# Triangular 16x16 blocks turned onto partitions and solved by VectorE, behind the attention queries' and keys' weight units

## The reference, cut to what matters

```python
def rwkv7_scan(r, decay, k, v, kk, a):
    def step(S, inp):
        r_t, w_t, k_t, v_t, kk_t, a_t = inp
        sa = jnp.einsum('bhij,bhj->bhi', S, -kk_t)
        S = (S * w_t[:, :, None, :]
             + sa[..., None] * (kk_t * a_t)[:, :, None, :]
             + v_t[..., None] * k_t[:, :, None, :])
        y = jnp.einsum('bhij,bhj->bhi', S, r_t)
        return S, y
...
def rwkv_attention_mixer(h, w_in, ...):
    proj = h @ w_in
    p_rwkv, q, k, v = jnp.split(proj, [RWKV_COLS, RWKV_COLS + ATT_WIDTH, RWKV_COLS + 2 * ATT_WIDTH], axis=-1)
    y_rwkv = rwkv7_group(p_rwkv, mu, ...)
    y_att = chunk_band_attention(q, k, v, rel_bias)
    return jnp.concatenate([y_rwkv, y_att], axis=-1) @ w_out
```

## Time and profile before

| | us |
|---|---|
| median of 3 runs (lowest, highest) | 949.78 (947.76, 949.82) |
| the profiled execution, its own time | 948.01 |
| its span | 946.2 |
| PE busy | 908.1 (96%) |
| PEld busy | 774.2 (82%) |
| DVE busy | 626.2 (66%) |
| ACT busy | 450.0 (48%) |
| POOL busy | 72.9 (8%) |
| mean granted TensorE clock, share of full speed | 0.981 |

### The profile page before, as it was taken

How to read it: one execution, slowest core, us unless ns; L and a number is a source line. 1 busy time by engine, 2 the same in 40 slices (tenths; PEclk the granted TensorE clock), 3 DMA queues, 4 the chain that set the end, 5 groups by cost and what they waited for, 6 DMA issues and landing times.

```text
span 946.2 us, 18298 instructions
## 1 busy us (share of the span) xinstructions
PE 908.1 (96%) x7834; PEld 774.2 (82%) x7834; DVE 626.2 (66%) x835; ACT 450.0 (48%) x641; POOL 72.9 (8%) x149
## 2 busy tenths in 40 slices
PE   8999999999999986799999999999999999999997
PEld 6888788899899975678788888888985688888886
DVE  5669788677768954365676565656756766665655
ACT  6555565434567442221364444445442655444453
POOL 6000000000120030000000000000653000000000
PEclk9999999999999996699999999999999999999999
DMA  9765444556665540010256655564884246566631
GB/s 326 248 199 162 148 164 135 178 179 188 224 201 170 187 135 5 4 47 13 74 159 233 192 178 180 199 200 147 251 234 124 70 140 214 185 206 195 199 105 45
DMA packets 106096, 152.41 MB, mean 161 GB/s; under 512 B 4114, under 2 KB 82464, under 8 KB 106016
## 3 DMA queue, kind: packets, MB, share of 16 engines
q1 hardware_dynamic: 101424, 140.99, 46.6%
q0 software_dynamic: 4272, 9.85, 3.7%
q10 hardware_dynamic: 320, 0.40, 0.1%
HBM read 145.38 MB, written 1.06 MB: 155 GB/s over the span
## 4 chain that ended last, share of the span: by engine, by line
PE 89%; DVE 4%; ACT 3%; issue 3%; DMA 1%; SPq 0%; DVEq 0%; ACTq 0%
PE banks L2011 20%; PE banks L1961 14%; PE banks L1963 14%; PE banks L1962 14%; PE banks L2012 10%; PE banks L2661 3%; PE banks L2357 2%; DVE wl L1126 1%; PE banks L2074 1%; PE banks L2128 1%; PE banks L2377 1%; PE banks L2513 1%; ACT wh L676 1%; DMA raw<-in_w_in 1%; PE banks L2152 1%
## 5 line engine op out<-in xcount | busy, mean ns | idle before, releaser
L1126 DVE TENSOR_TENSOR wl<-raw,wh 128x2048 fp32r<-128x2048 f32 x130 | 297.3, 2290 | 108.9 <-ACT wh L676 108.4
L2011 PE MATMUL banks<-x,wh 128*128 128x512 f32 x896 | 315.9, 395 | 1.2 <-DVE x L1194 1.1
L676 ACT ACTIVATE wh<-raw 128x2048 fp32r<-128x2048 f32 x132 | 252.4, 1913 | 132.7 <-PE banks L1963 90.5
L2012 PE MATMUL banks<-x,wl 128*128 128x256 f32 x896 | 250.6, 280 | 0.0
L2011 PEld LDWEIGHTS banks<-x,wh 128*128 128x128 f32 x896 | 168.2, 188 | 42.1 <-issue 4.9
L2012 PEld LDWEIGHTS banks<-x,wl 128*128 128x128 f32 x896 | 168.4, 188 | 1.2
L1961 PE MATMUL banks<-wh,yh 128*128 128x512 f32 x290 | 114.0, 393 | 1.8 <-DVE yl L1715 1.3
L1963 PE MATMUL banks<-wh,yl 128*128 128x512 f32 x290 | 112.5, 388 | 0.0
L1962 PE MATMUL banks<-wl,yh 128*128 128x512 f32 x290 | 112.5, 388 | 0.0
L1961 PE MATMUL banks<-x,wh 128*128 128x256 f32 x320 | 91.9, 287 | 1.8 <-DVE x L1194 1.7
L1962 PE MATMUL banks<-x,wh 128*128 128x256 f32 x320 | 89.9, 281 | 0.0
(11 more groups left out here) (364 smaller groups left out, 1180.3 us busy)
## 6 DMA issues: line engine op xcount, KB each, us to landing
raw<-in_l_ffn_up SPq DMA_DIRECT2D x32, 1024.0 KB, 5.5
raw<-in_l_ffn_down SPq DMA_DIRECT2D x32, 1024.0 KB, 5.0
raw<-in_w_in SPq DMA_DIRECT2D x29, 1024.0 KB, 5.4
raw<-in_l_w_in SPq DMA_DIRECT2D x13, 1024.0 KB, 5.3
raw<-in_l_pw SPq DMA_DIRECT2D x12, 1024.0 KB, 6.1
arena<-arena POOLq DMA_DIRECT2D x64, 71.0 KB, 4.5
raw<-in_w_out SPq DMA_DIRECT2D x4, 1024.0 KB, 5.0
raw<-in_l_w_out SPq DMA_DIRECT2D x4, 1024.0 KB, 5.0
```

Source lines behind the costliest of these rows:

```text
L676: nc.scalar.activation(wh[:, u % WBUFS, :], raw[:, u % RAWS, :], ACT.Copy).then_inc(E("hi_split"), 1)
L1126: nc.vector.tensor_tensor(wl[:, u % WBUFS, :], raw[:, u % RAWS, :], wh[:, u % WBUFS, :].bitcast(F32), ALU.subtract).then_inc(E("lo_split"), 1)
L2011: mm(outs[t], h[:, k, c], x2[:, k, :, :].rearrange("p w t -> p (w t)"), start=k == 0, stop=False)
L2012: ins = mm(outs[t][:, 0:T], l[:, k, c], xh[:, k, :], start=False, stop=k == KC - 1)
```

## The change

The series N2, D2, N4, D4, X2, D8, X4, X8 and the Gram product GD are gone from PE. GN and GA move up behind `q2_1` and behind `bo`. DVE masks GN into N1, transposes it in 32x32 blocks so that each partition holds one 16x16 triangle (`blocks_turned`), solves the two 8x8 triangles in it by substitution with small operations over at most 24 elements (`solve_eighths`), joins them (`join_eighths`) and transposes the result back into X (`blocks_returned`); another transpose of N1, masked by GpSimd, gives ET. The scaling of kHat and bHat goes from DVE to GpSimd, that of the bonus term from DVE to ACT. EX and the attention's first step come between the two halves of `v2`, and the attention's steps are dealt anew among AV, Z1, ZZ. Cut to its core:

```diff
@@ plan()
-    t_units("q2_", "l0_w_in_2", Q2, 2)
+    s.unit("T", "l0_w_in_2", 0, Q2, s.use("q2_0"))
     s.use("nat_vn0", 2), s.use("nat_vn1", 3)
+    s.unit("T", "l0_w_in_2", 0, Q2 + 256, s.use("q2_1"))
+    s.use("GN0", 6), s.use("GN1", 7)
     s.unit("T", "l0_w_in_2", 0, K2, s.use("k2_0"))
     s.use("bo0", 4), s.use("bo1", 5)
+    s.use("GA0", 6), s.use("GA1", 7)
+    s.use("nat_kn0", 2), s.use("nat_kn1", 3)
     s.unit("T", "l0_w_in_2", 0, K2 + 256, s.use("k2_1"))
@@ gpsimd, behind the band's memset
+            pool.wait_ge(E("k_scaled"), 1)
+            nc.gpsimd.tensor_tensor(by_chunk(kHat), by_chunk(kTil), pcb, ALU.mult).then_inc(E("k_hat_ready"), 1)
+            wait_full(pool, "bo1")
+            pool.wait_ge(E("b_scaled"), 1)
+            nc.gpsimd.tensor_tensor(by_chunk(bHat), by_chunk(bTil), pcb, ALU.mult).then_inc(E("b_hat_ready"), 1)
+            pool.wait_ge(E("cross_turned"), 1)
...
+            nc.gpsimd.tensor_tensor(by_chunk(ET), by_chunk(ET), cross, ALU.mult).then_inc(E("cross_ready"), 1)
@@ scalar
+            for c in range(4):
+                nc.scalar.activation(chunks(rk)[:, c, :], chunks(rk)[:, c, :], ACT.Copy, scale=vcol("l0_r_k_2", c))\
+                    .then_inc(E("bonus_terms"), 1)
@@ vector: new functions
+            def blocks_turned():
...
+                mark(nc.vector.transpose(turned, by_halves(N1)))
+                sync()
+                parts = turned.rearrange("p (j b i) -> p j b i", b=2, i=16)
+                mark(nc.vector.scalar_tensor_tensor(out=series.rearrange("p (j i) -> p j i", i=16), in0=parts[:, :, 0, :],
+                                                    scalar=parity[:, 0:1], in1=parts[:, :, 1, :], op0=ALU.mult, op1=ALU.add))
...
+            def solve_eighths():
+
+                for m in range(1, 7):
+                    n = 7 - m
...
+                    sync()
+                    mark(nc.vector.tensor_tensor(term, column, row, ALU.mult))
+                    sync()
+                    mark(nc.vector.tensor_tensor(rest, rest, term, ALU.add))
...
+            def join_eighths():
...
+                mark(nc.vector.reduce_sum(sums, terms, AX_X))
...
+            def blocks_returned():
...
+                nc.vector.transpose(by_halves(X), turned).then_inc(E("inverse_ready"), 1)
+                nc.vector.transpose(ET, N1).then_inc(E("cross_turned"), 1)
@@ vector: the order (the five other passes over 128x1024 are in it too)
+            next_unit()
+            scaled_out(q2[:, 0:2, :], "q2_0")
...
+            blocks_turned()
+            dve.wait_ge(E("bonus_product"), 1)
+            nc.vector.tensor_tensor(kTil, kTil, Pinv, ALU.mult).then_inc(E("k_scaled"), 1)
             next_unit()
             scaled_out(q2[:, 2:4, :], "q2_1")
+            solve_eighths()
+            next_unit()
+            for par in range(2):
+                masked(AK, f"GA{par}", par)
             scaled_out(k2[:, 0:2, :], "k2_0")
+            join_eighths()
+            dve.wait_ge(E("b_scaled"), 1)
+            blocks_returned()
             next_unit()
             scaled_out(k2[:, 2:4, :], "k2_1")
+            nc.vector.tensor_tensor(rTil, rTil, Pc, ALU.mult).then_inc(E("r_scaled"), 1)
+            next_unit()
+            dve.wait_ge(E("band_ready"), 1)
+            wait_empty(dve, "k2_1")
+            scores(16), scores(17)
             wait_full(dve, "v2_1")
@@ tensor: behind the queries' and keys' units
+            t_unit("q2_1")
+            pe.wait_ge(E("b_scaled"), 1)
+            gram("GN", bTil, aTil)
+            t_unit("k2_0")
...
+            pe.wait_ge(E("k_scaled"), 1)
+            gram("GA", kTil, aTil)
+            pe.wait_ge(E("k_hat_ready"), 1)
+            transposes("kn", kHat)
+            t_unit("k2_1")
+            pe.wait_ge(E("b_hat_ready"), 1)
+            transposes("bn", bHat)
+            nat_unit(("v2_0", "v2_1"), 0)
+            pe.wait_ge(E("inverse_ready"), 1)
+            pe.wait_ge(E("cross_ready"), 1)
+            cross_products()
...
+            heads_step(0, 16, 8)
+            nat_unit(("v2_0", "v2_1"), 1)
+            transposes("an", aTil)
...
+            values_first(0), values_first(1)
+            heads_step(2, 16, 8)
...
+            solve_first(0)
+            wait_empty(pe, "v2_0"), wait_empty(pe, "v2_1")
+            heads_step(3, 16, 8)
+            solve_first(1)
+            heads_step(4, 16, 8)
+            solve_second(0)
+            heads_step(5, 16, 8)
+            solve_second(1)
+            heads_step(6, 16, 8)
...
+            states_transposed(0)
+            heads_step(7, 16, 8)
+            heads_step(8, 16, 8)
+            heads_step(9, 16, 8)
```

More of the change, by code:

```diff
@@ L1605, in _ @@
+            scores(20), scores(21)
+            solved("ZZ", 0)
+            probabilities(20), probabilities(21)
+            heads_out(5, 16)
+            solved("ZZ", 1)
+            scores(22), scores(23)
+            heads_out(7, 16)
+            probabilities(22), probabilities(23)
+            heads_out(9, 16)
             next_unit()
@@ L2304, in _ @@
                     unfold_rows("kn_b", rk)
-            t_unit("q2_0")
-            t_unit("q2_1")
-            pe.wait_ge(E("rows_mixed"), len(RW_ORDER))
-            transposes("vn", slot(2))
-            t_unit("k2_0")
-            pe.wait_ge(E("bonus_terms"), 4)
-            for i in range(2):
-                give(mm(take(f"bo{i}"), head_ones, rk[:, 512 * i:512 * i + 512], start=True, stop=True), f"bo{i}")
-            t_unit("k2_1")
-            nat_unit(("v2_0", "v2_1"), 0)
-            pe.wait_ge(E("scaled_keys"), 2)
-            transposes("kn", kHat)
-            nat_unit(("v2_0", "v2_1"), 1)
-            pe.wait_ge(E("scaled_keys"), 4)
-            transposes("bn", bHat)
-            transposes("an", aTil)
             def htile(ap, tt, h):
@@ L2338, in gram @@
             def gram(name, left, right):
-                outs = [take(f"{name}{par}_0") for par in range(2)]
+                outs = [take(f"{name}{par}") for par in range(2)]
                 for p in range(4):
@@ L2347, in gram, with cross_products @@
                 for par in range(2):
-                    give(last[par], f"{name}{par}_0")
-            def blocks(name, left, right):
-                out = take(f"{name}0_0")
+                    give(last[par], f"{name}{par}")
+            def cross_products():
+                out = take("EX")
                 for h in range(16):
@@ L2356, in blocks @@
                         r = chunk_rows(i)
[L2357 to L2358 removed]
+                        ins = mm(out[r, cols], ET[r, cols], X[r, cols], start=True, stop=True)
+                give(ins, "EX")
             def values_first(tt):
[L2362 removed]
+                out = take(f"AV{tt}")
                 for h in range(8):
@@ new lines, in _ @@
+            t_unit("q2_0")
+            pe.wait_ge(E("rows_mixed"), len(RW_ORDER))
+            transposes("vn", slot(2))
+            t_unit("q2_1")
+            pe.wait_ge(E("b_scaled"), 1)
+            gram("GN", bTil, aTil)
+            t_unit("k2_0")
+            pe.wait_ge(E("bonus_terms"), 4)
+            for i in range(2):
+                give(mm(take(f"bo{i}"), head_ones, rk[:, 512 * i:512 * i + 512], start=True, stop=True), f"bo{i}")
+            pe.wait_ge(E("k_scaled"), 1)
+            gram("GA", kTil, aTil)
```

303 lines of the change are left out of this document (119 added, 184 removed), and 4 rows, old and new, of the table BLOCK_SERIES.

## The result

| | before | after |
|---|---|---|
| median of 20 runs each, same chip, us | 950.56 | 945.04 |
| lowest, highest | 947.49, 960.56 | 934.25, 952.58 |
| profiled execution, us | 948.01 | 949.54 |
| its mean granted clock | 0.981 | 0.967 |

After over before is 0.9895, with a 95% interval of 0.9865 to 0.9924: faster by 1%, where 3% was forecast, and outside the range of 913 to 934. The profiled execution of after is one of the longer ones of its 20, so its 949.54 is not to be set against the median. How long one takes goes with its mean granted clock: 934.25 us at 0.984, 938.31 at 0.979, 941.6 at 0.974, 945.92 at 0.969, 948.54 at 0.965, 952.58 at 0.962.

The account below looks back on a forecast made before the run. PE was taken to bound the kernel, busy 908.1 of 946.2 us. The scan beginning at 385.1 instead of 413.12 took 28.0 from 948.0, giving 920.0; 1.8 for the median made 921.8, rounded 922, range 913 to 934.

Parts of the forecast that it names:

- What bounds, what is removed: PE bounds; dropping the series and GD frees 26.9 us, of which 15 are pauses, waits and low clock.
- GN, GA and EX as single bursts of 1.3: Moved between weight units on PE, each takes 1.3 us without a pause; upper end 3.8.
- EX can go at 343.5: PE reaches EX at 343.5 us, with DVE's X and GpSimd's mask for ET ready by 343.
- These transposes or strided passes have no row: DVE's new passes before EX: priced at 0.68 us like the 512-element row; upper bound twice, 7.8 us more.
- DVE is late: Rival before EX: new passes cost double or GpSimd slows them, so PE waits; about 930 us, chance 0.17.
- The closing stage: From EX to the scan: AV ends at 355.5, three softmax pairs at 7.5 us, wait 1.2, tail 3.9: 383.1.
- The 2.0 that the sum added for clock and lateness: Added before the scan: 1.3 us for one pair at 1.2 GHz, 0.7 for a slightly late DVE.
- 385.1: Forecast start of the scan in us, against 413.12 before: 28.0 us less.
- What follows is unchanged code, with buffers as full as before: From the scan on: nothing changes, so the 28.0 us gained before it leave 920.0 for the profiled execution.
- Its rival at 1.2 GHz: The closing stage runs at 1.2 GHz and 8 us a pair: about 929 us, chance 0.12.
- the rival that had feared 10 us: Slow block transposes on DVE: the change turns slower at about 10 us each, near 955 at 12; chance 0.04.

Follow-up runs that it names:

- run 8: Changed kernel plus 512 independent 32x32 products that nothing reads, between AV and attention step 2: 970.99 us, 1.0225 of before.
- run 7: Changed kernel with the scalings of kHat and bHat moved from GpSimd back to DVE: 947.13 us, no ratio given.
- run 11: Run 5 with the fillers of run 9, kHat and bHat on DVE, and ET's transpose and mask early, behind N1's: 925.96 us, 0.9753 of before.
- run 3: Changed kernel with ET's mask on DVE, behind the transposes, instead of GpSimd: 937.01 us, 0.9871 of before.
- run 12: Run 11 with EX in PSUM bank 1 instead of 0 and k2_1 copied out ahead of DVE's unit split: 921.44 us, 0.97 of before.
- run 9: Changed kernel plus 512-column matmuls that nobody reads: three before attention step 8, one before step 9, one before the scan: 929.46 us, 0.9793 of before.
- run 10: Run 4 with six matmuls that nobody reads before attention step 8, filling its gap: 954.66 us, 1.0064 of before.
- run 1: Changed kernel plus four 512-column matmuls that nobody reads before attention step 8: 934.2 us, 0.9846 of before.
- run 6: Run 5 plus matmuls that nobody reads: three before EX, three before attention step 8, one before step 9, one before the scan: 926.66 us, 0.9759 of before.
- run 4: Kernel before the change, with 18 dependent memsets on DVE making PE idle before attention step 8: 960.11 us, 1.0103 of before.
- run 2: Changed kernel with ACT's copies of step 7's output and wt0 ahead of the last two exponentials: 930.7 us, 0.9801 of before.
- run 5: Run 2 with DVE's split of the next unit moved ahead of heads_out(9): 932.21 us, 0.9838 of before.

## Why the prediction was wrong

It forecast 922 us and got 945.04. By its own steps:

- **What bounds, what is removed: right.** The pauses were the supply of instructions, as far as run 8 shows it. The Trainium skill, Runtime: NRT & Kernel Launch, section Instruction fetch mechanics, has the crossing of a block mostly hidden; run 8 disagrees with 14.9 us in 8 pauses.
- **GN, GA and EX as single bursts of 1.3: right.** 1.29, 1.29, and 1.93 for EX at 1.2 GHz, behind its idle time.
- **EX can go at 343.5: 5.0 us off** beside the 2 us that the execution was late by. "These transposes or strided passes have no row" was said, and the lower bound taken because every row had the same time per element; but all those rows read in order. The four strided passes cost 1.05 to 1.09 for 0.68, together 1.6. Two small operations cost 2.8 more beside GpSimd. kHat took 3.92 for 2.34, so the transposes waited 1.3, and the mask took 3.22 for 1.2, so EX waited 3.67. This was the rival "DVE is late", given 0.17. The Trainium skill, GPSIMD Engine Reference, section Specifications, has GpSimd share its SBUF interfaces with VectorE and contend with VectorE's instructions with two SBUF inputs; the sum set that aside, and runs 7 and 11 agree with it (a gain of 2.8 us where GpSimd left, a split of 3.37 where it came). The wait for bank 0, which ended only 0.5 us before the mask, was in no case (runs 3, 12).
- **The closing stage: nearly right.** From EX's start to AV's end 13.0 us for 12.0; three pairs with the wait for `heads_out(7)` 24.5 for 23.7; the tail 5.0 for 3.9, at the low clock. The 2.0 that the sum added for clock and lateness belong against these. 2.1 + 5.0 + 1.0 + 0.8 + 1.1 - 2.0 is the 8.0 us by which the scan began later than 385.1.
- **"What follows is unchanged code, with buffers as full as before": this is the step that failed.** The code is unchanged, the clock isn't. The prediction saw the 4 us of idle PE behind step 7 and charged 1.3 us for it, up to where the scan begins. It cost 19.0 in the profiled execution: from 393.12 to 440.69 are 47.6 us, from 413.12 to 441.68 were 28.6. Its rival at 1.2 GHz ended at the scan as well. In the kernel before the clock had been at 0.50 to 0.97 through the same stage, from 356 to 404, and was at 1.00 before the scan, which hid the risk. Runs 9, 10, 1 and 6 show the cause by filling the gap, run 4 by making one.

With the clock back before the scan (run 9, 929.46) about 7 us over the forecast are left. The second fault accounts for much of them: the scan begins at 391.35 in run 9, where 385.1 was forecast, and at 384.01 in run 12, which has neither fault and takes 921.44. How much is its own can't be told, since run 12 also has the orders of runs 2 and 5 and five fillers; that it is close to 922 is partly luck.

What stays open: what decides, from one execution to the next, how long the clock stays low. In the traces it lasted until about 438 in after, 424 in run 1, 399 in run 2 and 464 in run 4, with a PE that was mostly busy behind the gap. No run varied this alone.

## What to carry to other kernels

Behind a stage that leaves TensorE idle for a few microseconds, cost the stage after it as well, at half the clock: the gap itself was 4.8 us here, its price up to 19. Where the wait can't be taken away, a few matmuls that nobody reads, placed ahead of the wait, filled idle time and were worth 10 to 14 us (run 9). Placed behind one of two waits they delay the work instead (run 6). And an operation whose elements are strided, or which stands beside a busy GpSimd, has no price from rows in which neither holds; nor is a wait gone before the next one behind it has been looked up, bank and all.

## What the runs showed that was not expected

- **A busy PE may stay at 1.2 GHz for a long time.** In after PE was busy for 4.00 of 4 us in window after window from 404 to 436 at 0.50. With small products, full rows of busy time did not bring the clock back there, while in run 2 the same scan had it back within 10 us of its start. The Trainium skill, TensorE: Matmul & The Clock Gate, section HAM oscillation, describes the clock falling in a kernel's waits and coming back behind them, over and over; here it came back late, which makes one gap dearer than its length.
- **Small VectorE operations may stand until GpSimd's is done.** Three did: those of 12 elements above, and the softmax's negation of 128x2:

```profile
366.86 1.77 DVE L1283 TENSOR_SCALAR small<-small 128x2 f32<-128x2 f32 x1
```

The median of its 16 in the trace is 0.17 us. This one ended at 368.63; GpSimd's pass of 2.35 us beside it began at 366.25 and ended at 368.60. In run 7, where that pass is still on GpSimd, it takes 1.77 again and ends within 0.05 us of the pass. Removing GpSimd's work was tried for the first two alone (run 7); why these stand while long passes beside GpSimd mostly keep their 2.29 us was not.
- **A block transpose is cheap.** 0.66 us for 128x512 of fp32, and 1.07 with a stride of 64 B: the rival that had feared 10 us was far off.
